# Expert results of a two-layer trunk: rows stored to DRAM and fetched per token, in place of scatter products into a transposed sum

## The chip, the cores and the metric

One core of a Trainium2 chip. The metric is the time of one execution on the device in microseconds (us), the median of several runs. All data are float32.

## What is computed

A trunk of two layers over 264 tokens (256 of a prompt, 8 single ones), 1024 channels. The change touches only the last stage, the mixture of experts: each token goes to the two best of eight experts, its results are weighted and added to the residual, and a last RMS norm follows.

```python
def swiglu(h, wg, wu, wd):
    return (jax.nn.silu(h @ wg) * (h @ wu)) @ wd

def moe_swiglu(h, router, wg, wu, wd):
    logits = (h @ router).astype(jnp.float32)
    top_v, top_i = lax.top_k(logits, TOP_K)
    gates = jax.nn.softmax(top_v, axis=-1)
    out = jnp.zeros_like(h)
    for e in range(N_EXPERTS):
        gate_e = jnp.sum(jnp.where(top_i == e, gates, 0.0), axis=-1)[..., None].astype(h.dtype)
        out = out + gate_e * swiglu(h, wg[e], wu[e], wd[e])
    return out
...
            x = x + mix
            x = x + moe_swiglu(rmsnorm(x, p['norm_ffn_odd'][i]), p['moe_router'][i], p['moe_w_gate'][i],
                               p['moe_w_up'][i], p['moe_w_down'][i])
    y = rmsnorm(x, p['final_norm'])
```

Each expert has gate and up weights of 1024 x 2816 and down weights of 2816 x 1024.

## The kernel before

The engines run programs of their own and meet at semaphores that are written out by hand. The expert stage is a sequence of items, one expert each: `moe_item(s, t)` with `s` from 0 to 6 written out, and `s` = 7 (`STATIC`) in a loop whose count comes from the routing; with this data the loop runs once. An item has a fixed number of slots for tokens, `SEQ_CAP` = 64, 96, 64, 96, 64, 128, 64, 64, and the experts are put in an order in which they fit.

**Weights.** SyncE loads an expert as 24 pieces (`load_piece`, L617): 8 for gate, 8 for up (1.44 MB each), 8 for down. They go round a ring of 33792 columns x 128 partitions. A piece of the second half of an expert is loaded over pieces of the first half, and so on, each load waiting on `w_used`, which PE raises when it has done with a piece (`LAST_OVER`).

**An item on PE.** Eight gate chunks (L2278, L2272 or L2264, by the number of slots), with work for other items slipped in between them: after chunk 1 the transposes of this item's gates and three small products that give the token numbers of the next item (`turn_gates`, L2172 and L2177, into bank 4); after chunks 2 to 5 one block each of `scatter` (L2200, L2208 or L2211). Then eight up chunks, transposes of the activations (L2299), transposes of the next item's rows (L2163), and the down products (L2317, L2328), whose result lies by slot: rows are tokens, columns are channels.

**What becomes of a result.** ScalarE and VectorE copy it out of PSUM into `ysb` (L1093, L1683, L1685). The next item's `scatter` multiplies it with the one-hot gate matrix `SelGT` (and `SelXT` where the item had 96 slots), so that a product of 128 channels x 264 tokens comes out, weighted. VectorE adds eight of these per item to `accT`, the transposed residual (`scattered`, L1636 and L1638). In the last item `sum_rows` (L2219) transposes `accT` back into the banks of `LAST_BANK` between up and down pieces. They stay open there (`mark_sums`, L2225, tells the accumulation state), and after the loop PE adds the last item's result on top (L2408). ScalarE squares the banks and VectorE writes the normed output from them.

**Rows.** The normed tokens stand in DRAM as `hrows`. For each next item VectorE writes the token numbers to `rowidx` (L1619) and POOL fetches the rows with an indirect DMA (`fetch_rows`, L784).

Of the kernel before, what the change touches and what calls it, by code (L numbers as in the profile page):

```python
# [32 lines left out]
SCAT = DC // 2  # L33
# [185 lines left out]
def bank_uses():  # L219
# [3 lines left out]
    for s in range(EXP + 1):  # L223
# [9 lines left out]
        item["selT"] = use(4, 5) if s and SEQ_CAP[s - 1] == 96 else use(4)  # L233
        if s:
            item["scat"] = use(4, 5)
            for _ in range(SCAT - 1):
                use(4, 5)
# [7 lines left out]
STEP5 = USES[EXP]["start"][1] - USES[EXP - 1]["start"][1]  # L245
EXIT_BASE = [sum(len(EXITS[SEQ_CAP[k]]) for k in range(s)) for s in range(EXP)]
# [5 lines left out]
def build(nc, i, o):  # L252
# [5 lines left out]
    with ctx:  # L258
# [185 lines left out]
        SelX = reg(19136, BLK * P).rearrange("p (k j) -> p k j", k=BLK)  # L444
        SelXT = reg(19520, BLK * P)
        iota32 = reg(20416, P)
# [3 lines left out]
        rowidx = sb("rowidx", 1, I32)  # L450
        hrows = nc.dram_tensor("hrows", [T, D], F32).ap()

# [66 lines left out]
        def _(sp):  # L519
# [99 lines left out]
            def first_expert():  # L619

                of = weights_of(slice(FIRST_EXPERT, FIRST_EXPERT + 1))
                for at in EARLY:
# [4 lines left out]
                    if at == RING_PIECES - 1:  # L627
                        sp.wait_ge(sem("t_full4"), 1)
                        sp.wait_ge(sem("t_full5"), 1)
                        sp.wait_ge(sem("hrows_stored"), 48)  # L630
# [23 lines left out]
            sp.wait_ge(sem("ord_ready"), 2)  # L654
# [15 lines left out]
        def _(pool):  # L670
# [3 lines left out]
            def then(ins):  # L674
# [32 lines left out]
                            pattern=[[0, DC], [-1, P]], channel_multiplier=1).then_inc(sem("wsn_ready"), 1)  # L707
# [50 lines left out]
            g.iota(iota32, pattern=[[0, 4], [1, P // 4]], base=64, channel_multiplier=0,  # L758
                   allow_small_or_imprecise_dtypes=True).then_inc(sem("route_const"), 1)
# [46 lines left out]
        def _(act):  # L806
# [28 lines left out]
            act.wait_ge(sem("wsn_ready"), 1)  # L835
# [29 lines left out]
            a.activation(arep, arep, ACT.Exp).then_inc(sem("arep_exp"), 1)  # L865
# [8 lines left out]
            a.activation(dtx[0:TS, 16:32], adt[0:TS, 32:48], ACT.Exp).then_inc(sem("sda_ready"), 1)  # L874
# [41 lines left out]
            act.wait_ge(sem("tot_ready"), 2)  # L916
# [30 lines left out]
            a.activation(Z, Z, ACT.Silu).then_inc(sem("z_ready"), 1)  # L947
# [96 lines left out]
            for k in range(BLK):  # L1044
                act.dma_start(hrows[P * k:P * k + ROWS[k], :], htok[0:ROWS[k], k, :]).then_inc(sem("hrows_stored"), 16)

# [6 lines left out]
            def moe_item(s, t):  # L1053
# [29 lines left out]

                for part in EXITS[cap]:
# [1358 lines left out]
```

## Time and profile before

| | |
|---|---|
| time, median of 3 runs | 1320.86 us (1320.65 to 1324.37) |
| the profiled execution | 1327.41 us, its span 1325.7 us |
| mean granted clock of TensorE | 0.987 of full speed |
| PE busy | 1299.6 us, 98% |
| VectorE, ScalarE, POOL busy | 373.8, 169.9, 61.0 us |
| DMA moved | 380.81 MB, mean 287 GB/s |
| gate and up products for 64 slots (L2278) | 280.9 us, 1792 instructions |
| down products (L2317) | 176.1 us, 704 instructions |
| adds into `accT` (L1636) | 12.0 us, 28 instructions, 429 ns each |

PE is the matmul queue. Each float32 product is recorded as two instructions. The ends of matmuls are modelled, so that an engine shown as busy may in part be waiting. The DMA share is the mean share of time in which the core's 16 DMA engines move something, GB/s what they moved. The queue q1 carries SyncE's loads, q10 ScalarE's DMAs, q0 those of POOL. The expert stage fills the second half of the span, from about 658 us on; its items begin on PE at 658, 721, 820, 886, 985, 1051, 1172 and 1241 us.

### The profile page before, as it was taken

Reading aid. Unit: us, or ns where it says so; the run is one execution under the profiler, and the core shown is the slowest. Engines: PE = TensorE matmul, PEld = TensorE weight load, DVE = VectorE, ACT = ScalarE, POOL = GpSimd, SP = SyncE. Lnnn points to the kernel's source line nnn. Section 1 sums busy time; section 2 is a strip of 40 time slices with the busy share of each in tenths; the row PEclk is TensorE's granted clock in tenths of the full one; section 3 lists DMA queues with packets and bytes.
Section 4 is the critical chain, followed back from the end, with each engine's and each line's share of the span. In section 5 each row is a group of like instructions: output and inputs, shape, how many; then the busy total and the mean of one; then the engine's idle time right before and its main releaser. Section 6 shows DMA issues by size and latency. Waiting matters only on the chain.

```text
span 1325.7 us, 17071 instructions
## 1 busy us (share of the span) xinstructions
PE 1299.6 (98%) x7217; PEld 826.4 (62%) x7217; DVE 373.8 (28%) x869; ACT 169.9 (13%) x367; POOL 61.0 (5%) x87
## 2 busy tenths in 40 slices
PE   8999999999999999999999999999999999999997
PEld 6878788888888888867843433434334444444452
DVE  5537775421111113984400110011100110110101
ACT  2241423010000100013200000000000000101002
POOL 1013110000000201100000000000000000000000
PEclk8999999999999999999799999999999999999999
DMA  8639633565456424354699999999999999899994
GB/s 289 206 130 304 221 96 96 191 179 168 127 166 223 143 72 127 132 198 197 267 388 424 408 424 425 408 424 410 424 425 424 424 406 425 323 359 418 409 423 188
DMA packets 105484, 380.81 MB, mean 287 GB/s; under 512 B 7580, under 2 KB 62796, under 8 KB 80778
## 3 DMA queue, kind: packets, MB, share of 16 engines
q1 hardware_dynamic: 97811, 359.46, 69.9%
q0 software_dynamic: 3216, 11.54, 2.7%
q10 hardware_dynamic: 4386, 8.76, 2.1%
q8 instruction: 57, 0.93, 0.3%
q14 instruction: 14, 0.11, 0.0%
HBM read 371.96 MB, written 8.86 MB: 287 GB/s over the span
## 4 chain that ended last, share of the span: by engine, by line
PE 89%; DVE 7%; ACT 1%; DMA 1%; SPq 1%; issue 1%; DVEq 0%; ACTq 0%
PE ps L1746 30%; PE ps L2278 21%; PE ps L2317 13%; PE ps L2264 6%; PE ps L2272 3%; DVE both L1450 3%; PE ps L1999 3%; PE ps L2328 2%; PE ps L2299 1%; PE ps L1991 1%; PE ps L1977 1%; PE ps L2211 1%; PE ps L2148 1%; PE ps L2200 1%; DMA both<-in_w_in_even_dram 1%
## 5 line engine op out<-in xcount | busy, mean ns | idle before, releaser
L1746 PE MATMUL ps<-both 128*128 128x264 f32 x2080 | 474.3, 390 | 0.5 <-DMA both<-in_w_in_even_dram 0.3
L1746 PEld LDWEIGHTS ps<-both 128*128 128x128 f32 x2080 | 397.0, 192 | 72.3 <-issue 2.7
L2278 PE MATMUL ps<-both 128*64 128x384 f32 (+1 forms) x1792 | 280.9, 466 | 0.8 <-ACT both L1050 0.8
L2278 PEld LDWEIGHTS ps<-both 128*64 128x64 f32 x1792 | 127.0, 138 | 152.6 <-issue 142.7
L2317 PE MATMUL ps<-both 128*64 128x512 f32 (+1 forms) x704 | 176.1, 596 | 0.0
L2317 PEld LDWEIGHTS ps<-both 128*64 128x64 f32 (+1 forms) x704 | 58.5, 143 | 98.6 <-issue 97.8
L1653 DVE TENSOR_TENSOR both<-both,ps 128x384 f32<-128x384 f32 (+7 forms) x46 | 20.9, 485 | 233.2 <-PE ps L2278 118.1
L2264 PE MATMUL ps<-both 128*128 128x510 f32 (+1 forms) x192 | 77.2, 559 | 0.0
L2264 PEld LDWEIGHTS ps<-both 128*128 128x128 f32 x192 | 35.9, 189 | 39.8 <-issue 32.5
L1450 DVE SCALAR_TENSOR_TENSOR both<-both,par 128x256 f32<-128x256 f32 x120 | 50.9, 481 | 1.0
L2272 PE MATMUL ps<-both 128*32 128x384 f32 (+1 forms) x512 | 47.1, 465 | 0.0
L1064 ACT ACTIVATE both<-ps 128x384 f32<-128x384 f32 (+7 forms) x46 | 19.0, 437 | 213.9 <-PE ps L2278 113.2
L1081 ACT ACTIVATE both<-ps 128x384 f32<-128x384 f32 (+1 forms) x28 | 12.5, 463 | 185.7 <-PE ps L2299 185.6
L784 POOL DMA_INDIRECT both<-hrows,rowidx x8 | 8.5, 1058 | 602.5 <-DVE rowidx L1619 345.0
L1999 PE MATMUL ps<-both 128*128 128x264 f32 x160 | 35.8, 386 | 0.0
L1636 DVE TENSOR_TENSOR both<-both,ps 128x264 f32<-128x264 f32 x28 | 12.0, 429 | 82.4 <-PE ps L2211 52.7
L1393 DVE TENSOR_TENSOR both<-both,ps 128x264 f32<-128x264 f32 x16 | 6.9, 429 | 99.9 <-PE ps L1746 70.0
L1999 PEld LDWEIGHTS ps<-both 128*128 128x128 f32 x160 | 30.4, 190 | 5.2
L1685 DVE COPY both<-ps 64x512 f32<-64x512 f32 x5 | 3.5, 694 | 101.9 <-PE ps L2317 101.9
L818 ACT ACTIVATE both<-both 128x264 f32<-128x264 f32 x32 | 12.8, 419 | 144.2 <-DVE both L1393 114.6
L1683 DVE COPY both<-ps 128x512 f32<-128x512 f32 x3 | 2.1, 692 | 98.8 <-PE ps L2328 60.8
L2272 PEld LDWEIGHTS ps<-both 128*32 128x32 f32 x512 | 14.3, 109 | 23.8 <-issue 22.7
(369 smaller groups left out, 882.4 us busy)
## 6 DMA issues: line engine op xcount, KB each, us to landing
both<-in_moe_w_gate_dram SPq DMA_DIRECT2D x64, 1408.0 KB
both<-in_moe_w_up_dram SPq DMA_DIRECT2D x64, 1408.0 KB
both<-in_moe_w_down_dram SPq DMA_DIRECT2D x48, 1536.0 KB
both<-in_w_in_even_dram SPq DMA_DIRECT2D x10, 2048.0 KB
both<-in_moe_w_down_dram SPq DMA_DIRECT2D x16, 1024.0 KB
both<-in_ffn_w_gate_dram SPq DMA_DIRECT2D x11, 1024.0 KB
both<-in_ffn_w_up_dram SPq DMA_DIRECT2D x11, 1024.0 KB
both<-in_ffn_w_down_dram SPq DMA_DIRECT2D x4, 2816.0 KB
```

Source lines behind the costliest of these rows:

```text
L1064: a.activation(act_view(p0, p1, r, a0, nb, q0, q1), exit_view(GATE_BANKS[cap][bank], p0, p1, nb, q0, q1, at), ACT.Silu).then_inc(sem("moe_ ...
L1450: ins = v.scalar_tensor_tensor(out=dst, in0=ca[:, c, k:k + TP], scalar=col("conf_dw_w", 8 * k + c), in1=dst, op0=ALU.mult, op1=ALU.add)
L1653: v.tensor_tensor(to, to, exit_view(UP_BANKS[cap][bank], p0, p1, nb, q0, q1, at), ALU.mult).then_inc(sem("moe_mul"), 1)
L1746: ins = mm(ps[:, 0:T], w[:, c, cols:cols + P], src[:, c, :], start=c == 0, stop=c == nk - 1)
L1977: mm(psum[at % RING][:, 0:T], w[:, c, P * (n % 2):P * (n % 2) + P], mix[:, c, :], start=c == DC, stop=False)
L1991: ins = mm(ahead[n][:, 0:T], out_w[n][:, c, P * (n % 2):P * (n % 2) + P], mix[:, c, :], start=False, stop=c == DC - 1)
L1999: ins = mm(ps[:, 0:T], w[:, c, P * (n % 2):P * (n % 2) + P], mix[:, c, :], start=c == DC, stop=c == DC - 1)
L2264: ins = mm(ps[:, 0:n], xg[:, c, 0:P], w[:, HALF * r + first:HALF * r + first + n], start=c == 0, stop=c == DC - 1)
L2272: ins = mm(ps[rows:rows + 32, 0:WIDE[k]], xg[:, c, 64:96], w[:, first:first + WIDE[k]], start=c == 0, stop=c == DC - 1)
L2278: ins = mm(ps[64 * r:64 * r + 64, 0:WIDE[k]], xg[:, c, 0:64], w[:, first:first + WIDE[k]], start=c == 0, stop=c == DC - 1)
L2317: ins = mm(out, lhsT, w[:, b - b0, 512 * h:512 * (h + 1)], start=b + r == 0, stop=b + r == 11)
L2328: ins = mm(psum[7][at:at + 32, :], hT32[:, k % 2, b - b0, k // 2, r, :], ws[r][:, b - b0, 512 * h:512 * (h + 1)], start=b == 0, stop=b == 10)
```

## The change

The results of items 0 to 6 no longer pass through scatter products.

- **Store.** When `ysb` holds an item's result, ScalarE stores it to a new DRAM buffer `yrows`, unweighted: one DMA of 128 rows for the item with 128 slots, two of 64 half rows for 64 slots, four for 96. A row of zeros stands at its start. The next overwriting of `ysb` waits for these stores (`y_put`). The result of an item with 96 slots is folded together on ScalarE and VectorE first.
- **Choice.** After item 0 VectorE works out for each token the two rows of `yrows` that hold its results, and their gates (`results_chosen`); a token whose expert is item 7 gets the zero row there.
- **Fetch.** POOL fetches them by six indirect DMAs (`fetch_results`), two rounds over 128, 128 and 8 tokens, ahead of its last fetch of rows. The first round waits for item 6's store, each DMA of the second for the adds of the first.
- **Add.** VectorE adds them, weighted, to `sums`, the residual by token, before it enters its loop for item 7 (`results_added`).
- **Residual.** PE transposes `accT` in items 0 to 2 after gate chunk 3 (`turn_sums`), and ScalarE and VectorE copy it to `sums`. `sum_rows` and `mark_sums` go.
- **Item 7.** Its gates are transposed after up chunk 1. Its six products stand at the end of the loop's body and open the banks anew; VectorE adds them to `sums`, and the squares and the output are taken from `sums`.
- Gate matrices are built for item 7 alone. `iota32` and `SelXT` go, and several semaphores of earlier stages are merged into others with the same order of work.

```diff
+            def fetch_results(m, k):
+
+                n, at = ROWS[k], 1 + BLK * m + k
+                if m:
+                    pool.wait_ge(sem("y_added"), k + 1)
+                pool.indirect_dma_start(
+                    out=yback[k][0:n, :], out_offset=None, in_=yrows[:, :],
+                    in_offset=bass.IndirectOffsetOnAxis(ap=rowidx[0:n, at:at + 1], axis=0)).then_inc(sem("y_back"), 16)
+
             pool.wait_ge(sem("crw_stored"), 32)
-            pool.wait_ge(sem("hrows_stored"), 48)
+            pool.wait_ge(sem("hrows_stored"), 64)
             for s in range(STATIC):
                 fetch_rows(s, 0)
-            pool.wait_ge(sem("ord_ready"), 2)
+            pool.wait_ge(sem("y_chosen"), 1)
+            pool.wait_ge(sem("y_put"), PUT_BASE[STATIC])
+            for m in range(2):
+                for k in range(BLK):
+                    fetch_results(m, k)
+            pool.wait_ge(sem("ord_ready"), 3)
             items = pool.value_load(tint[0:1, 0:1], min_val=1, max_val=ITEMS)
             with pool.Fori(0, items) as t:
                 fetch_rows(STATIC, t)
...
+                if s:
+                    act.wait_ge(sem("y_put"), PUT_BASE[s])
                 a.activation(ysb[0:n, 0:512], psum[6][0:n, :], ACT.Copy).then_inc(sem("ysb_lo"), 1)
+                if cap == 96:
+                    for h in range(2):
+                        a.activation(ysb[64 * h:64 * h + 32, 512:1024], psum[7][64 * h + 32:64 * h + 64, :],
+                                     ACT.Copy).then_inc(sem("ysb_lo"), 1)
+                if s < STATIC:
+                    act.wait_ge(sem("ysb_lo"), LO_BASE[s + 1])
+                    act.wait_ge(sem("ysb_hi"), s + 1)
+                    first = ROW_BASE[s]
+                    if cap == P:
+                        act.dma_start(yrows[first:first + P, :], ysb[:, :]).then_inc(sem("y_put"), 16)
+                    else:
+                        for h in range(2):
+                            act.dma_start(yrows[first:first + 64, 512 * h:512 * h + 512],
+                                          ysb[64 * h:64 * h + 64, 0:512]).then_inc(sem("y_put"), 16)
...
+            def results_added():
+
+                dve.wait_ge(sem("t_free4"), USES[BLK - 1]["res"][0] + 1)
+                dve.wait_ge(sem("t_free5"), USES[BLK - 1]["res"][1] + 1)
+                n = 0
+                for m in range(2):
+                    dve.wait_ge(sem("y_back"), 48 * (m + 1))
+                    if m:
+                        dve.wait_ge(sem("y_added"), BLK)
+                        dve.wait_ge(sem("sums_added"), BLK)
+                    for k in range(BLK):
+                        rows = ROWS[k]
+                        for h in range(2):
+                            to = sums[k][h][0:rows, :]
+                            v.scalar_tensor_tensor(out=to, in0=yback[k][0:rows, 512 * h:512 * h + 512],
+                                                   scalar=gsel[0:rows, 3 * m + k:3 * m + k + 1], in1=to, op0=ALU.mult,
+                                                   op1=ALU.add).then_inc(sem("y_added" if h else "sums_added"), 1)
...
+                dve.wait_ge(sem("t_full4"), t * STEP4 + (USES[s]["ids"][0] + 1))
+                rows_known(s, t)
+                dve.wait_ge(sem("rows_known"), t + (s + 1))
+                dve.sem_inc(sem("t_free4"), 1)
...
-                    scattered(t * STEP4 + USES[s]["scat"][0], t * STEP5 + USES[s]["scat"][1])
...
+                if s == STATIC:
+                    gates_turned(t * STEP4 + USES[s]["gates"][0])
...
+                    dve.wait_ge(sem("banks_read"), t * 6 + 6)
+                    for k in range(BLK):
+                        n = ROWS[k]
+                        for h in range(2):
+                            dve.wait_ge(sem("psum_full"), t * 6 + (len(TILES) + 2 * k + h + 1))
+                            to = sums[k][h][0:n, :]
+                            v.tensor_tensor(to, to, psum[LAST_BANK[k][h]][0:n, :], ALU.add).then_inc(
+                                sem("banks_read"), 1)
...
+            results_added()
+            dve.wait_ge(sem("y_added"), 2 * BLK)
+            dve.wait_ge(sem("sums_added"), 2 * BLK)
             items = dve.value_load(tint[0:1, 0:1], min_val=1, max_val=ITEMS)
             with dve.Fori(0, items) as t:
                 moe_item(STATIC, t)
...
+                for h, count in enumerate((n4, n5)):
+                    pe.wait_ge(sem(f"t_free{4 + h}"), count)
+                    for j in range(4):
+                        ins = tr(psum[4 + h][0:n, P * j:P * (j + 1)], accT[:, 4 * h + j, P * k:P * k + n], ident[:, :])
+                    ins.then_inc(sem(f"t_full{4 + h}"), 1)
...
-                    if s and 2 <= c < 2 + SCAT:
-                        scatter(SEQ_CAP[s - 1], t + s, t * STEP4 + USES[s]["selT"][0], t * STEP4 + USES[s]["scat"][0],
-                                t * STEP5 + USES[s]["scat"][1], (c - 2,))
+                        row_ids(SEQ_CAP[min(s + 1, EXP - 1)], t + (s + 2), t * STEP4 + USES[s]["ids"][0])
+                    if c == 3 and s < BLK:
+                        turn_sums(s, *USES[s]["res"])
                 for c in range(DC):
                     chunk(1, c)
                     if s == STATIC and c == 1:
-                        pe.wait_ge(sem("t_free4"), t * STEP4 + (USES[s]["scat"][0] + SCAT))
-                        pe.wait_ge(sem("t_free5"), t * STEP5 + (USES[s]["scat"][1] + SCAT))
-                        pe.wait_ge(sem("moe_silu"), t * XEXITS + (EXIT_BASE[s] + 4))
-                        sum_rows(0, 1)
-                    if s == STATIC and c == 2:
-                        sum_rows(1, 1)
+                        turn_gates(t + 1, t * STEP4 + USES[s]["gates"][0])
...
+                if s == STATIC:
+                    pe.wait_ge(sem("t_free5"), t * STEP5 + (USES[s]["gather"][1] + 1))
+                    pe.wait_ge(sem("t_free4"), t * STEP4 + (USES[s]["gates"][0] + 1))
+                    pe.wait_ge(sem("ysb_lo"), t + (LO_BASE[s] + 1))
+                    pe.wait_ge(sem("ysb_hi"), t + (s + 1))
+                    for k in range(BLK):
+                        n = ROWS[k]
+                        for h in range(2):
+                            mm(psum[LAST_BANK[k][h]][0:n, :], SelGT[64 * h:64 * h + 64, P * k:P * k + n],
+                               ysb[64 * h:64 * h + 64, 0:512], start=True, stop=True).then_inc(sem("psum_full"), 1)
```

## Rows read from the trace of the kernel before

**Rows 1.** Page, part 2: DMA share in 40 slices of the span, in tenths.

```profile
DMA  8639633565456424354699999999999999899994
```

**Rows 2.** Windows by item: us, busy by engine, PEclk, DMA share, GB/s.

```profile
984.80:1051.20 66.40, 66.40 (x408) 29.91 (x408) 8.80 (x23) 4.63 (x10) 0.96 (x1) 1.00 1.01 425
1051.20:1172.40 121.20, 121.20 (x337) 57.56 (x339) 10.21 (x31) 7.68 (x23) 0.94 (x1) 1.00 0.94 380
1172.40:1238.00 65.60, 65.52 (x388) 29.36 (x388) 8.46 (x23) 4.44 (x11) 0.93 (x1) 1.00 1.00 410
1238.00:1312.20 74.20, 73.39 (x457) 35.49 (x457) 8.03 (x22) 4.49 (x10) 0.96 (x1) 1.00 0.91 374
```

**Rows 3.** Timeline of PE, item 2: start us, us, operation, count.

```profile
828.44 1.16 PE L2200 MATMUL ps<-both 64*128 64x264 f32 x8
829.53 2.59 PE L2278 MATMUL ps<-both 128*64 128x384 f32 x16
```

**Rows 4.** Timeline of PE in item 5, and the chain of work there.

```profile
1060.67 0.49 PE L2172 MATMUL ps<-ident,both 128*128 128x128 f32 x3
...
1066.45 0.72 PE L2211 MATMUL ps<-both 64*128 64x264 f32 x4
...
1072.02 0.72 PE L2211 MATMUL ps<-both 64*128 64x264 f32 x4
...
1083.88 47.46 PE ps L2264 x120
```

**Rows 5.** Page, part 3: packets, MB, share of 16 engines' span.

```profile
q0 software_dynamic: 3216, 11.54, 2.7%
q10 hardware_dynamic: 4386, 8.76, 2.1%
```

**Rows 6.** Windows of 20 and 12 us around row fetches, columns as before.

```profile
700.00:720.00 20.00, 20.00 (x101) 7.09 (x100) 0.56 (x1) 1.96 (x5) 0.00 (x0) 1.00 1.01 424
720.00:740.00 20.00, 20.00 (x161) 8.54 (x159) 4.92 (x16) 0.59 (x1) 1.83 (x1) 1.00 1.01 400
990.00:1002.00 12.00, 12.00 (x85) 6.24 (x85) 3.96 (x14) 0.00 (x0) 0.96 (x1) 1.00 1.01 422
```

**Rows 7.** POOL's row fetches: their line, and the time to landing.

```profile
L784 POOL DMA_INDIRECT both<-hrows,rowidx x8: 907/952/1832, 667.2 to 1248.2; - x8
...
DMA to landing us min/median/max: 8.5/8.9/9.8
```

**Rows 8.** Windows at the end of the weight stream, columns as before.

```profile
1304.00:1305.00 1.00, 1.00 (x10) 0.83 (x10) 0.00 (x0) 0.00 (x0) 0.00 (x0) 1.00 0.64 270
1305.00:1306.00 1.00, 1.00 (x6) 0.29 (x4) 0.00 (x0) 0.00 (x0) 0.00 (x0) 1.00 0.20 82
```

**Rows 9.** Timeline of the end, from PE's last piece to the last store.

```profile
1310.28 1.94 PE L2317 MATMUL ps<-both 128*64 128x512 f32 x8
...
1312.27 0.69 DVE L1685 COPY both<-ps 64x512 f32<-64x512 f32 x1 [23.37 <-PE ps L2317]
...
1313.60 2.95 PE L2408 MATMUL ps<-both 64*128 64x512 f32 x12
...
1314.76 0.60 ACT L1110 ACTIVATE both<-ps 128x512 f32<-128x512 f32 x1 [0.39 <-PE ps L2408]
...
1315.56 0.15 DVE L1704 TENSOR_SCALAR both<-both 128x1 f32<-128x1 f32 x1 [2.02 <-ACT both L1110]
...
1316.59 1.41 DVE L1711 SCALAR_TENSOR_TENSOR both<-ps,both 128x512 f32<-128x512 f32 x2
...
1322.16 0.34 SPq L666 DMA_DIRECT2D out_y_sample_dram<-both  x1
```

**Rows 10.** Timeline of PE, item 7: the first group of sums.

```profile
1268.96 1.16 PE L2219 MATMUL ps<-ident,both 128*128 128x128 f32 x8
```

**Rows 11.** Windows of PE at the lower clock: us, busy, PEclk, DMA, GB/s.

```profile
646.00:662.00 16.00, 15.22 (x65) 0.50 0.89 350
1322.00:1324.00 2.00, 0.00 (x0) 0.50 0.23 61
```

More of the change, by code:

```diff
@@ L32 @@
 XROUNDS = 4
-SCAT = DC // 2
 PIECES = 24
@@ L232, in bank_uses @@
         item = {"start": tuple(at)}
[L233 to L237, printed above, removed]
+        item["ids"] = use(4)
+        if s < BLK:
+            item["res"] = use(4, 5)
+        if s >= STATIC:
+            item["gates"] = use(4)
         item["gather"] = use(4, 5)
@@ L245 @@
 STEP5 = USES[EXP]["start"][1] - USES[EXP - 1]["start"][1]
+ROW_BASE = [1 + sum(SEQ_CAP[:s]) for s in range(STATIC)]
+YROWS = 1 + sum(SEQ_CAP[:STATIC])
+PUTS = {64: 2, 96: 4, P: 1}
+PUT_BASE = [16 * sum(PUTS[SEQ_CAP[k]] for k in range(s)) for s in range(EXP)]
+LO_BASE = [sum(3 if SEQ_CAP[k] == 96 else 1 for k in range(s)) for s in range(EXP)]
 EXIT_BASE = [sum(len(EXITS[SEQ_CAP[k]]) for k in range(s)) for s in range(EXP)]
@@ L1082, in columns @@
                     ins.then_inc(sem("ht_ready"), 1)
+                if s < BLK:
+                    if s == 0:
+                        act.wait_ge(sem("hrows_stored"), 64)
+                        act.wait_ge(sem("crw_stored"), 32)
+                    act.wait_ge(sem("t_full4"), USES[s]["res"][0] + 1)
+                    n = ROWS[s]
+                    a.activation(sums[s][0][0:n, :], psum[4][0:n, :], ACT.Copy).then_inc(sem("t_free4"), 1)
                 for part in EXITS[cap]:
@@ L1108, in _ @@
                 for h in range(2):
[L1109 to L1110 removed]
+                    act.wait_ge(sem("banks_read"), items * 6 + (2 * k + h + 1))
+                    a.activation(fsq[0:n, 512 * h:512 * (h + 1)], sums[k][h][0:n, :], ACT.Square,
                                  accum_out=ssum[0:n, 2 * k + h:2 * k + h + 1]).then_inc(sem("fin_sq"), 1)
@@ L1698, in _ @@
                 moe_item(STATIC, t)
-            gates_turned(items * STEP4 + (USES[EXP]["start"][0] - STEP4))
             dve.wait_ge(sem("fgain_loaded"), 16)
@@ L2215, in sum_rows @@
-            def sum_rows(k, h):
-                n = ROWS[k]
-                for j in range(4):
-                    mm(psum[LAST_BANK[k][h]][0:n, P * j:P * (j + 1)], accT[:, 4 * h + j, P * k:P * k + n], ident[:, :],
-                       start=j == 0, stop=False)
-            def mark_sums(opened):
-                for b, n in ((0, P), (1, P), (2, P), (3, P), (7, TS)):
-                    mm(psum[b][0:n, 0:1], ones[0:1, 0:n], ones[0:1, 0:1], start=opened, stop=not opened)
+                pe.wait_ge(sem("sel_ready"), chosen)
@@ new lines, in row_ids, with turn_gates @@
+                for b in range(BLK):
+                    ins = mm(psum[4][0:cap, BLK * P:BLK * P + 1], Sel[:, b, 0:cap], tokid[:, b:b + 1], start=b == 0,
+                             stop=b == BLK - 1)
+                ins.then_inc(sem("t_full4"), 1)
+            def turn_gates(value, n4):
+                pe.wait_ge(sem("t_free4"), n4)
+                pe.wait_ge(sem("selg_ready"), value)
+                for b in range(BLK):
+                    ins = tr(psum[4][:, P * b:P * (b + 1)], SelG[:, b, :], ident[:, :])
+                ins.then_inc(sem("t_full4"), 1)
@@ L2301, in turn_act, with down @@
                     ins.then_inc(sem("t_act"), 1)
-                def down(k, between=None):
+                def down(k):
                     b0, b1 = SEGS[k]
```

234 lines of the change are left out of this document (90 added, 144 removed).

## The prediction

> **What bounds the kernel now.** I read the page first: PE is busy for 98% of the span, but a busy PE in this profile may still be waiting inside a matmul, so this settles nothing. The line of DMA shares is full from the 20th slice on [rows 1]. Both could bound the expert part. So next came a table of windows cut where PE changes from one item (one expert with its slots) to the next [rows 2]. It gives DMA at a share of 1.01 and 410 to 425 GB/s in every item but the sixth (`s` = 5, 128 slots), where it falls to 380.
>
> Then I counted bytes backwards. One expert's weights are 3 x 1024 x 2816 x 4 B = 34.6 MB. After 1051.2 us the windows move 380 x 121.2 + 410 x 65.6 + 374 x 74.2 = 100.7 MB, of which 0.8 MB are three row fetches, so 99.9 MB of weights. Items 5 to 7 need 103.8 MB. At PE's start of item 5 the weight stream is thus only 3.9 MB ahead. By the same count it is 10.8 MB ahead at 984.8, 15.1 MB at 1172.4 and 7.1 MB at 1238.0. The ring holds 33792 columns, 17.3 MB. So DMA runs without a gap up to item 5. In item 5 PE needs 121.2 us where the stream needs 34.6/0.425 = 81 us, the ring fills, and SyncE can load only what PE releases. After that the stream is full again to its last byte, near 1305.3 [rows 8].
>
> PE's timeline says the other half. In item 2 a block of scatter products takes a slot of 829.53 - 828.44 = 1.09 us [rows 3] and otherwise the chunks follow each other evenly. PE never shows a gap for weights. So today PE sets the time, with the stream just behind it. There are two tight places, the start of item 5 and the end. How tight: of the 3.9 MB, 1.44 MB are the first piece itself, and the other 2.5 MB are 5.8 us at 425 GB/s. At the end PE's last piece, 1.94 us long, starts at 1310.28 [rows 9], 5.0 us after the stream's last byte. From both comes the time between a piece's last byte and PE's start. The trace bounds it by the last output store, from its issue at 1322.16 to the end of the span at 1325.7, 3.5 us with the issue in it, and by nothing from below. I take 2.5, nearer to the one row there is. Slack: 3.3 us at item 5, 2.5 us at the end.
>
> The Trainium skill, "DMA: Bandwidth & Descriptors", section "Anatomy of one DMA", gives about 2.0 us of fixed cost, mostly the wait until the last byte is confirmed. By that the two slacks would be 3.8 and 3.0 us, and the result 1 us lower.
>
> **Part by part, PE.** Removed are four scatter blocks in each of items 1 to 7. The block costs 5.57 us from one block to the next against 4.75 us for a bare chunk in item 5 [rows 4], so 0.8 us, and 1.1 us where the item before had 96 or 128 slots. That is 16 x 0.8 + 12 x 1.1 = 26 us, with the gate transposes of items 1 to 6 (about 0.4 us each, rows 4) and six groups of sums at about 1.1 us [rows 10] about 35 us. Added are eight transposes of `accT` in each of items 0 to 2, 1.1 us each time by the same row, and one gate transpose in item 7. If PE alone set the time this would be -30 us.
>
> It isn't, since the stream can't be hurried. Before item 5 PE gains about 14 us over items 0 to 4 but may use only the 3.3 us of slack: term **-3.3**. Item 5 itself stays bound by PE (about 117 us against 81), and there the removal counts in full: 4 x 0.82 + 0.42 for the three gate transposes [rows 4]: **-3.7**. Items 6 and 7 follow the stream again, whose restart hangs on PE's releases in item 5, so what PE saves in them gives only the slack at the end: **-2.5**.
>
> **DMA.** Stored are 576 rows of 4 KB, 2.36 MB, fetched 528 rows, 2.16 MB. Items 0 to 3 store 320 rows, 1.31 MB, ahead of item 5: full price. Item 4's 64 rows fall into item 5, where the stream waits for PE: free. Item 5's 128 rows (0.52 MB) come at its end, where the stream is still partly waiting: half. Item 6's 64 rows (0.26 MB) and all fetches fall into item 7, where it is full. That makes 1.83 MB of stores and 2.16 MB of fetches at some price p per MB. The lowest is the full rate, 1/0.425 = 2.35 us. The highest is from a fetch of 64 rows, where the 20 us around it moved 400 instead of 424 GB/s [rows 6]: 0.48 MB lost and 0.26 MB moved, 1.75 us for 0.26 MB, 6.7 us per MB. A fetch of 128 rows (990 to 1002) moved 422 against 425, so it cost 2.5 us per MB, and four of the six new fetches are of 128 rows. Between them lie the queues' own shares [rows 5]: ACT's queue, which will carry the stores, 2.1% of 1325.7 us for 8.76 MB, 3.2 us per MB; POOL's queue 2.7% for 11.54 MB, 3.1. I take these, since they are near the 128-row fetch and leave something for the 64-row pieces. 1.83 x 3.2 + 2.16 x 3.1 = **+12.6**.
>
> The Trainium skill's same page, section "Specifications", puts the SBUF side of DMA at 435 GB/s at most; the stream already has 425. By that rule the new bytes come on top at 2.3 us per MB and the sum below would be +2.3 instead of +5.7. It speaks against this change as the rows do.
>
> **The end.** Today PE goes from the last piece over 0.64 us of transposes to six final products, ACT squares each from PSUM, and DVE writes the first output at 1316.59. In the change the transposes are gone, but DVE must first add all six product tiles into `sums`, and the output steps stand behind all six in its queue. From PE's end at 1312.2: copy out to 1312.96, first product ready 1.16 us later [rows 9], six adds at 0.70 us (as L1711 and L1685 take) to 1318.35, then 1.03 us from the half step to the first output: 1319.4 against 1316.59. The later outputs keep their pace. The adds for 8 tokens may be shorter, so I take **+2.6**.
>
> Sum: -3.3 - 3.7 - 2.5 + 12.6 + 2.6 = **+5.7 us** against the profiled execution (1327.41 us, span 1325.7). The runs shown have a median of 1320.86, 6.5 less, and I put the same difference on it: **1326.6 us**.
>
> **Taken at nothing.** VectorE loses 56 adds and gains about 14 small steps after item 0; it idles for most of each item. Its wait for `y_back` is the exception, below. ScalarE's stores wait for VectorE's copy, and behind them stands only the next item's SiLU, a whole gate stage later. The waits on `y_put` are for stores tens of us old. The folding of the 96-slot result costs some 2 us on ACT and DVE, and the next item wants those banks later than that. POOL's fetches stand ahead of its fetch of rows for item 7's successor, whose result PE wants only after the up stage. Renamed semaphores cost nothing. The entry of the loop loses a 3 us marking step, hidden behind the stream.
>
> **Rivals.** (1) *The bytes slip in.* With p the whole sum is -6.9 + 3.99 p. It turns negative below p = 1.7 us per MB. That happens if writes to DRAM go beside reads, and fetched rows use gaps that a share of 1.01 doesn't show. At p = 0: -6.9, **1314.0**. For it: stores are the first large writes in this stage, and no row shows one under a full stream. Against: no fetch cost less than the full rate. Chance 0.17.
> (2) *Dear bytes.* All at the 64-row price, +19.8, **1340.7**; only the stores of 64 and 96 rows (1.57 MB) at it, +5.5 more, **1332.1**. For it: those stores use half of the partitions, as that fetch did. Chance 0.13.
> (3) *PE waits for the fetched rows.* In item 7 DVE adds all fetched rows before it frees bank 4, and PE wants the bank behind the second up chunk. PE ends item 6 near 1230; copy and store some 5.5 us; three issues of 1 us and 8.9 us to landing [rows 7], and some 2 more since 1.06 MB share the queue: 1250; first adds and the second round about 15 us more; adds 4.2 us: 1270. PE comes there with the stream at about 1265 and has 43.2 - 5.5 = 37.7 us of work behind it [rows 10], so it ends at 1308.6 with the new transposes, before the 1315.3 of my sum (1312.2 + 5.7 - 2.6). A wait of over 5 us may also cost clock: after PE's last product the granted clock falls to half, 0.50 in 1322 to 1324 [rows 11], 1.2 instead of 2.4 GHz. It stood there from 646 to 662 too, which would cost 8 us of PE work if all of such a stretch were needed; half of that I put to this case, and PE ends at 1312.6. The Trainium skill's "TensorE: Matmul & The Clock Gate", Part 1, says as much, that idleness brings the gate back to half rate. So the wait decides from a chain about 3 us longer than mine; 8 us longer gives 1320.6 for PE, 5.3 above the sum, **1331.9**. Chance 0.13.
> (4) *The change does not act*, for instance since the stream turns out not to be near its limit on both sides: about 1321, 0.03.
>
> **How the numbers follow.** My own case has 0.54, with p from 2.35 to 4.5 and the unknown latency from 0 to 3.5 us: 1319 to 1332. About 0.15 of it lies within 0.3% (4 us, about what a measurement of this kernel can tell from no change). Slower 0.39 + 0.13 + 0.13 = 0.65; within 0.15 + 0.03 + 0.03 = 0.21; faster 0.14. The range goes down into rival 1 and up over the milder form of rival 2: 1316 to 1336.
>
> **What would show it.** Item 5 takes 117 to 118 us instead of 121.2 and starts within 2 us of its old time, while items 2 and 4 show chunks spread to the stream's 3.4 us. The stream's last byte comes 4 to 8 us later, PE's last piece follows it by about 4.5 us, and the first output comes 7.2 us after PE's end instead of 4.4. Total DMA bytes rise by 4.5 MB. I am wrong if item 5 starts several us earlier than now (cheap stores), if PE shows a gap over 5 us early in item 7's up stage, or if PE's chunks stay at 2.4 us in item 4.

## The result, and the profile after

| | before | after |
|---|---|---|
| time, median | 1320.96 us (4 runs) | 1333.84 us (1331.44 to 1335.12, 4 runs) |
| ratio after / before | | 1.0089, 95% interval 1.0067 to 1.0112 |
| the profiled execution | 1327.41 us, span 1325.7 us | 1334.46 us, span 1332.7 us |
| mean granted clock | 0.987 | 0.983 |
| PE busy | 1299.6 us | 1263.3 us |
| DMA moved | 380.81 MB | 385.31 MB |

The change costs 12.9 us by the medians, 11.8 by the ratio; the forecast was 5.7 us, to 1326.6. PE's busy time fell by 36 us and the time still went up. Of these 36 us, 8 belong to the first profile of the kernel before: in the second one, below, PE is busy for 1291.5 us. So 28 us went, where the prediction counted about 30 net.

The page of the changed kernel, packets, MB and share of the 16 DMA engines by queue (before: [rows 5]). The new bytes stand where they were expected, 2.16 MB on POOL's queue and 2.37 MB on ScalarE's.

```profile
DMA  8639533574455433363899999999999999999992
...
q0 software_dynamic: 3856, 13.70, 3.1%
q10 hardware_dynamic: 5684, 11.13, 2.6%
```

Windows by item of the changed kernel, columns as in [rows 2]. The first row has the bounds of item 4 in the kernel before; in the changed kernel item 4 starts on PE at 975.0 us, and items 5, 6 and 7 at 1047.7, 1165.3 and 1225.1.

```profile
984.80:1051.20 66.40, 56.91 (x316) 23.19 (x313) 3.38 (x6) 4.62 (x10) 0.00 (x0) 1.00 1.01 425
1047.40:1165.00 117.60, 117.25 (x316) 56.27 (x316) 5.23 (x17) 7.08 (x21) 0.90 (x1) 1.00 0.99 403
1165.00:1225.00 60.00, 60.00 (x370) 35.43 (x371) 3.85 (x10) 4.42 (x10) 0.89 (x1) 1.00 1.01 408
1225.00:1316.70 91.70, 67.43 (x382) 29.77 (x378) 13.39 (x26) 4.58 (x10) 6.79 (x7) 0.87 0.89 363
```

The first row, most of it item 4, now shows PE waiting for the stream (of weights), 56.91 us busy of 66.40: PE begins the item nearly 10 us earlier than before and gives most of this back in waits. Item 5 takes 117.5 us where it took 121.2, as forecast. Item 6 is 5.6 us shorter too, 60.0 against 65.6. Then the last row: 24 us of 91.7 without PE, while the DMA share is not full either. What happens there stands in the waits of PE (line, what it waited for, us in total, times, longest) and in the chain of work that ended last (start us, us):

```profile
PE ps L2273 <- DVE both L1737: 18.8, 1, 18.8
PE ps L2373 <- DMA both<-in_moe_w_down_dram: 7.3, 12, 0.8
```

```profile
1216.52 8.76 PE ps L2373 x40
1226.56 9.42 DMA yrows<-both
1239.38 12.73 DMA both<-yrows,rowidx
1256.76 13.07 DMA both<-yrows,rowidx
1269.86 4.06 DVE both L1710 x6
1277.44 16.38 PE ps L2334 x96
```

PE stands still for 18.8 us at the last item's gate transposes (L2273), released by the gate matrices (L1737), which stand behind the second round of adds (L1710) in VectorE's program. The chain leads back over two rounds of fetches and the store of item 6's result. This is rival 3 of the prediction, with a chance of 0.13, and the time is within 2 us of the one it was given, 1331.9.

VectorE in the same stretch (timeline: start us, us, line, operation, [idle before <-releaser]), and POOL's fetches with their time to landing:

```profile
1252.25 4.05 DVE L1710 SCALAR_TENSOR_TENSOR both<-both 128x512 f32<-128x512 f32 x6 [26.26 <-DMA both<-yrows,rowidx]
1269.86 4.05 DVE L1710 SCALAR_TENSOR_TENSOR both<-both 128x512 f32<-128x512 f32 x6 [13.56 <-DMA both<-yrows,rowidx]
...
1275.63 0.86 DVE L1737 TENSOR_SCALAR both<-iota,both 128x128 f32<-128x128 f32 x3 [0.32 <-DVE rowidx L1671]
```

```profile
L804 POOL DMA_INDIRECT both<-yrows,rowidx x6: 885/946/1229, 1236.9 to 1256.8; - x6
```

The end of the changed kernel, against [rows 9]: the first row is the second half of PE's last down piece, which begins at 1314.8 and ends at 1316.7; the first output is written at 1323.11, and the last store is issued at 1328.70.

```profile
1315.70 1.03 PE L2373 MATMUL ps<-both 128*64 128x512 f32 x4
...
1318.76 3.67 DVE L1773 TENSOR_TENSOR both<-both,ps 128x512 f32<-128x512 f32 x6 [1.28 <-PE ps L2421]
...
1323.11 1.42 DVE L1804 SCALAR_TENSOR_TENSOR both<-both 128x512 f32<-128x512 f32 x2
...
1328.70 0.34 SPq L675 DMA_DIRECT2D out_y_sample_dram<-both  x1
```

### The profile page after: what moved, and what is told of

Same layout as the page of the kernel before. It is cut to its first block, busy times and chain, and to the rows that moved or that the text cites. A ratio compares the mean times of both kernels' runs of the same rounds, so it can differ in the third digit from the quotient of the medians.

```text
span 1332.7 us, 16652 instructions
## 1 busy us (share of the span) xinstructions
PE 1263.3 (95%) x7002; PEld 809.8 (61%) x7002; DVE 358.6 (27%) x814; ACT 174.3 (13%) x374; POOL 66.0 (5%) x108
## 2 busy tenths in 40 slices
DMA packets 107421, 385.31 MB, mean 289 GB/s; under 512 B 7965, under 2 KB 63181, under 8 KB 82716
## 4 chain that ended last, share of the span: by engine, by line
PE 77%; DMA 11%; DVE 7%; SPq 1%; ACT 1%; issue 1%; POOL 0%; DVEq 0%; ACTq 0%; POOLq 0%
PE ps L1839 30%; PE ps L2334 15%; PE ps L2373 10%; PE ps L2320 6%; DMA both<-in_moe_w_gate_dram 5%; PE ps L2328 3%; DVE both L1502 3%; PE ps L2092 3%; DMA both<-in_moe_w_up_dram 2%; DMA both<-yrows,rowidx 2%; PE ps L2382 2%; PE ps L2355 1%; PE ps L2084 1%; PE ps L2070 1%; DMA yrows<-both 1%
## 5 line engine op out<-in xcount | busy, mean ns | idle before, releaser
L2334 PEld LDWEIGHTS ps<-both 128*64 128x64 f32 x1792 | 136.6, 138 | 160.2 <-issue 125.2
L1445 DVE TENSOR_TENSOR both<-both,ps 128x264 f32<-128x264 f32 x16 | 6.9, 429 | 99.9 <-PE ps L1839 70.0
L843 ACT ACTIVATE both<-both 128x264 f32<-128x264 f32 x32 | 12.8, 419 | 144.4 <-DVE both L1445 114.6
L1000 ACT ACTIVATE both<-both 128x264 f32<-128x264 f32 x22 | 9.3, 423 | 139.3 <-DVE both L1474 139.3
L1464 DVE TENSOR_TENSOR both<-ps,rstd 128x264 f32<-128x264 f32 x22 | 9.5, 433 | 66.4 <-PE ps L1839 66.4
```

Of the source, the lines that this page charges most:

```text
L2334: ins = mm(ps[64 * r:64 * r + 64, 0:WIDE[k]], xg[:, c, 0:64], w[:, first:first + WIDE[k]], start=c == 0, stop=c == DC - 1)
```

## The experiments

Two theories at first. A: bytes and wait both count; the sum of the forecast holds, +5 to 6 us, and the wait puts its 6 to 7 us on top. B: one of the two is the whole loss, the other is hidden behind it.

**The kernel before, once more**, for a second profile: in the first one the granted clock was at half for 17 us at 646 us.

> The kernel before, unchanged, profiled once more. Its first profiled execution took 1327.4 us against a median of 1321, and shows 17 us at half clock from 646 us on, which the profile of the changed kernel does not have; there item 0 starts on PE at 651.6 instead of 658.1 us. Theory 'clock luck': the low stretch is not a property of the kernel; a second profile has none, its item 0 starts near 651.6 and its span is about 1319 us, so that the true distance of the two kernels in spans is some 13 us and not 7. Rival: the stretch belongs to the kernel before, and the changed kernel is free of it since some of its early steps moved; then the second profile has it again at 646 us and a span near 1325.7.

Measured: 1321.27 us (1318.57 to 1324.82), ratio 0.9987 [0.9972, 1.0002], and a span of 1320.1 us in its profile, 5.6 less than the first profile of the same kernel. The window that stood at PEclk 0.50 in [rows 11]:

```profile
646.00:662.00 16.00, 15.22 (x110) 9.11 (x111) 7.74 (x46) 3.16 (x4) 0.98 (x1) 1.00 0.83 320
```

Item 0 starts on PE at 649.2 instead of 658.1, item 5 at 1043.9 instead of 1051.1. So the profile on which the forecast rests was a late one by some 6 to 7 us. In this one PE already waits for weights at the start of item 5:

```profile
PE ps L2264 <- DMA both<-in_moe_w_gate_dram: 1.5, 1, 1.5
```

This profile is the one to compare the others with. Its chain of work, item 5's start, item 6's start and the last product and store:

```profile
1043.87 9.69 PE ps L2264 x24
...
1165.08 4.88 PE ps L2278 x32
```

```profile
1304.70 1.94 PE L2317 MATMUL ps<-both 128*64 128x512 f32 x8
...
1316.59 0.34 SPq L666 DMA_DIRECT2D out_y_sample_dram<-both  x1
```

**The wait taken away** (`split_adds`): the second round's adds go into item 7's work, behind the gate matrices.

```diff
-            def results_added():
+            def results_added(rounds):
...
-                for m in range(2):
+                for m in rounds:
...
                 moe_xg(SEQ_CAP[min(s + 1, EXP - 1)], t * STEP5 + USES[s]["gather"][1])
+                if s == STATIC:
+                    results_added((1,))
+                    dve.wait_ge(sem("y_added"), 2 * BLK)
+                    dve.wait_ge(sem("sums_added"), 2 * BLK)
...
-            results_added()
-            dve.wait_ge(sem("y_added"), 2 * BLK)
-            dve.wait_ge(sem("sums_added"), 2 * BLK)
+            results_added((0,))
```

> The changed kernel with only the order on VectorE changed: the adds of the second fetched round stand late in item 7, behind the copy of the next rows, and not ahead of the item. Same bytes, same adds. Theory 'PE waits' : PE reaches the gate transposes at 1257.7 us and waits to 1276.5 for VectorE; the first round is added by 1256.3, so the wait falls to about 1 us, PE follows the stream, whose last byte comes at 1306.3, and ends at 1306.3 + 2.5 + 1.9 = 1310.7 instead of 1316.7: -6 us, about 1328 us. The half clock of 1261 to 1281 goes as well. Rival 'bytes': the stream with its new bytes sets the end and the wait is hidden: within 1 us of 1333.8.

Measured: 1327.86 us (1323.83 to 1329.13), ratio 1.0038 [1.0023, 1.0052]. The wait is gone from PE's list, which is led by waits for weights, and the chain of work ends in the stream:

```profile
PE ps L2335 <- DMA both<-in_moe_w_up_dram: 16.5, 16, 3.3
PE ps L2374 <- DMA both<-in_moe_w_down_dram: 10.0, 16, 0.8
PE ps L2335 <- DMA both<-in_moe_w_gate_dram: 6.0, 5, 2.1
```

```profile
1045.43 9.69 PE ps L2321 x24
...
1162.94 4.88 PE ps L2335 x32
...
1225.35 42.86 DMA both<-in_moe_w_up_dram
1270.94 36.19 DMA both<-in_moe_w_down_dram
```

```profile
1307.18 1.94 PE L2374 MATMUL ps<-both 128*64 128x512 f32 x8 [0.40 <-DMA both<-in_moe_w_down_dram]
...
1321.10 0.34 SPq L675 DMA_DIRECT2D out_y_sample_dram<-both  x1
```

Taking the wait away, and the half clock that came with it, is worth 1333.8 - 1327.9 = 6.0 us (6.7 by the ratios). Theory A holds. What is left, by these rows against those of the kernel before: item 5 starts 1.6 later, takes 3.7 less, from item 6's start to the last product 4.6 more (144.2 against 139.6), from there to the last store 2.0 more (13.9 against 11.9). Sum +4.5; by the ratio it is +5.0.

**The fetches left out** (`no_fetch`) **and all new bytes left out** (`no_bytes`).

```diff
             for s in range(STATIC):
                 fetch_rows(s, 0)
-            pool.wait_ge(sem("y_chosen"), 1)
             pool.wait_ge(sem("y_put"), PUT_BASE[STATIC])
-            for m in range(2):
-                for k in range(BLK):
-                    fetch_results(m, k)
...
-            results_added()
-            dve.wait_ge(sem("y_added"), 2 * BLK)
-            dve.wait_ge(sem("sums_added"), 2 * BLK)
+            dve.wait_ge(sem("t_free4"), USES[BLK - 1]["res"][0] + 1)
+            dve.wait_ge(sem("t_free5"), USES[BLK - 1]["res"][1] + 1)
```

> The changed kernel without the six fetches and without their adds; the stores stay. The results of items 0 to 6 are left out of the output. Theory: the wait goes and 2.16 MB leave the full stream. At 2.35 to 3.1 us per MB the last byte comes 5.1 to 6.7 us earlier than 1306.3, and PE ends near 1304 to 1306 instead of 1316.7: 1321 to 1323 us. If a fetched MB costs 6.7 us, as a fetch of 64 rows did, the stream ends 14 us earlier and the time is 1314 to 1316. If fetched bytes are free, it is 1328, as with the adds split.

In the second kernel ScalarE's stores to `yrows` and the waits on `y_put` are gone as well. Both leave the results of items 0 to 6 out of the output.

> The changed kernel with neither stores nor fetches nor adds of fetched rows (the results of items 0 to 6 are left out of the output). Compared with the one without fetches it gives the price of the stores alone. Theory (3.2 us per MB for the 1.31 MB ahead of item 5, and about 0.5 MB behind it): 4 to 6 us less than without fetches, 1316 to 1318 us, with item 5 starting some 4 us before its 1047.7. Rival 'stores slip in beside reads': item 5 starts at the same time and the time is within 1.5 us of the one without fetches.

Measured: `no_fetch` 1319.35 us (1317.28 to 1322.29), ratio 0.9977 [0.9961, 0.9994]; `no_bytes` 1315.76 us (1314.03 to 1317.99), ratio 0.9950 [0.9936, 0.9963]. The last product of the down stage in each:

```profile
1300.70 1.94 PE L2368 MATMUL ps<-both 128*64 128x512 f32 x8 [0.39 <-DMA both<-in_moe_w_down_dram]
```

```profile
1295.24 1.94 PE L2350 MATMUL ps<-both 128*64 128x512 f32 x8 [0.40 <-DMA both<-in_moe_w_down_dram]
```

Between `split_adds` and `no_fetch` lie 6.5 us of the last product's start, and 8.5 us of the medians: 3.0 to 3.9 us for each of 2.16 MB. The 1321 to 1323 us that were expected put the fetches too low. Between `no_fetch` and `no_bytes` lie 5.5 us by the product and 3.6 us by the medians for the stores, 1.5 to 2.3 us for each of 2.36 MB. All new bytes together: 11.9 us by the product, 12.1 by the medians, where the forecast had 12.6. Rival 1, in which the bytes cost next to nothing, is refuted, and without its bytes the change would be a gain of 5.5 us (by the ratio 6.6).

**Where PE's removed work counts.** `ballast_others` and `ballast_item5` give back to PE, in `split_adds`, 16 products of 128 x 128 that nobody reads, once in five items around item 5 and once in item 5.

```diff
                     chunk(1, c)
+                    if s in (1, 2, 3, 4, 6) and 2 <= c < 6:
+                        if s < BLK and c == 2:
+                            pe.wait_ge(sem("t_free5"), USES[s]["res"][1] + 1)
+                        for _ in range(4):
+                            mm(psum[5][:, 0:P], ident[:, :], ones[:, :], start=True, stop=True)
```

> split_adds with the PE work of the removed scatter products given back in items 1, 2, 3, 4 and 6 only: in each, 16 products of 128 x 128 that nobody reads, four behind each of the third to sixth up chunks (about 1.1 us for four, so some 4.4 us an item, 22 us in all). If PE in these items waits for the stream of weights anyway, as the windows of the items say, the 22 us lie in its waits: the time stays within 1 us of split_adds, 1327.9, and item 6 starts within 1 us of 1163. The rival, in which PE is what sets the pace there and the removed products were worth their duration, gives 1327.9 + up to 22 = 1345 to 1350; every us of start of item 6 above 1163 is a us of PE that counted.

In the other kernel the first added line reads `if s == 5 and 2 <= c < 6:`.

> split_adds with the same 16 products in item 5 alone, the one item whose duration went from 121.2 to 117.5 us with the change. If item 5 is PE-bound, as the forecast has it, it takes 117.5 + 3.5 to 4.4 = 121 to 122 us, and the kernel 1331.4 to 1332.3. The rival, that item 5 had become bound by the stream (its DMA share is 0.99) and only part of the removed work was gained, gives item 5 117.5 to 119 us and the kernel 1328 to 1329.5.

Measured: `ballast_others` 1326.66 us (1326.23 to 1326.83), ratio 1.0049 [1.0032, 1.0065]; `ballast_item5` 1330.39 us (1328.17 to 1333.04), ratio 1.0083 [1.0062, 1.0105]. Five times as much work outside item 5 moves nothing that can be told from `split_adds`; it goes into PE's waits, which shrink:

```profile
PE ps L2335 <- DMA both<-in_moe_w_up_dram: 8.6, 4, 2.9
...
PE ps L2374 <- DMA both<-in_moe_w_down_dram: 2.1, 4, 0.8
```

In item 5 it costs 2.5 us against `split_adds` and 3.7 against `ballast_others` by the medians (4.5 to 5.9 by the ratios; its four runs lie at 1328.2, 1328.3, 1332.5 and 1333.0, so the size is loose), and the item takes 121.1 us instead of 117.5. The reason is that in this item the ring is full and the stream may load only what PE releases: between 1047 and 1165 us of `split_adds` SyncE's loads wait 95 of 118 us for PE to release pieces, between 1225 and 1306 only 8.6 of 81. So a slower PE slows the loads, as the window of the item shows, first `split_adds`, then `ballast_item5` (columns as in [rows 2]): 390 GB/s instead of 402.

```profile
1047.00:1165.00 118.00, 118.00 (x327) 56.45 (x327) 5.91 (x18) 7.67 (x22) 0.90 (x1) 1.00 0.98 402
```

```profile
1047.00:1165.00 118.00, 118.00 (x342) 58.40 (x340) 5.22 (x17) 7.07 (x21) 0.90 (x1) 1.00 0.97 390
```

**Does it matter when the bytes come?** `rest_first` fetches the results from items up to 5 while item 6 runs.

```diff
-                n, at = ROWS[k], 1 + BLK * m + k
+                n, at = ROWS[k], 1 + BLK * (1 - m) + k
...
-            pool.wait_ge(sem("y_put"), PUT_BASE[STATIC])
             for m in range(2):
+                pool.wait_ge(sem("y_put"), PUT_BASE[STATIC - 1 + m])
...
+                if s == STATIC - 1:
+                    results_added((0,))
+                if s == STATIC:
+                    results_added((1,))
```

> Same stores and same fetched bytes as split_adds, but the round that needs no row of item 6 (each token's result from an item up to 5) is fetched and added already while item 6 runs, and only the other round waits for item 6's store and is added late in item 7. By the theory that only bytes are left to pay once PE waits for no added row, it gives the time of split_adds, 1327.9, within 1 us, with the fetch packets of the first round in item 6. The rival, that the burst of fetches behind item 6 delays the last item's weights more than the same bytes earlier do, gives 1323 to 1326.

Measured: 1326.48 us (1324.97 to 1327.89), ratio 1.0047 [1.0030, 1.0064]. The first round of fetches was issued from 1177.7 us on instead of 1234.6, the second at 1231.9 instead of 1251.8, and the time is that of `split_adds`, so no cost of the burst behind item 6 shows once PE doesn't wait for it.

**PE kept busy during the wait** (`wait_busy`, from the changed kernel):

```diff
                     if s == STATIC and c == 1:
+                        for _ in range(64):
+                            mm(psum[5][:, 0:P], ident[:, :], ones[:, :], start=True, stop=True)
                         turn_gates(t + 1, t * STEP4 + USES[s]["gates"][0])
```

> The changed kernel with 64 products of 128 x 128 that nobody reads ahead of the last item's gate transposes, where PE stands still for 18.8 us until the fetched rows are added; they take 17.4 us at the full clock. The wait itself stays as long, since its end is set by the fetches. If the granted clock of 0.50 after the wait (1261.0 to 1281.5 us in the changed kernel) is a matter of PE having stood still, it goes, and with it the 4 us of work at half clock behind the wait: 1333.8 - 2 = 1331.8, or as much as 1 us more or less. If the whole loss is the wait, 1333.8 within 0.5. If the dummy products run past the wait's end, 0 to 3 us more.

Measured: 1334.43 us (1332.27 to 1335.13), ratio 1.0109 [1.0092, 1.0126]: no gain. PE's windows across the wait and just behind it (us, busy, PEclk, DMA share, GB/s), first the changed kernel, then this one:

```profile
1261.00:1277.00 16.00, 0.46 (x2) 0.50 1.02 412
1277.00:1282.00 5.00, 5.00 (x21) 0.55 1.01 384
```

```profile
1261.00:1276.00 15.00, 11.17 (x97) 0.97 1.01 411
1276.00:1279.00 3.00, 3.00 (x12) 0.58 0.98 409
```

With PE at work through most of the wait, the granted clock stayed up there, so the half clock of the changed kernel did come from PE standing still. But the products took 14.6 us, less than the 17.4 expected, PE then stood for another 3.8 us, and the clock fell for 3.4 us all the same, from 1275.1:

```profile
1256.67 14.56 PE L2400 MATMUL ps<-ones,ident 128*128 128x128 f32 x128
1275.06 0.89 PE L2273 MATMUL ps<-ident,both 128*128 128x128 f32 x3 [3.83 <-DVE both L1737]
```

So the kernel got back under 1 us of PE work, which the times can't show. How the 6.0 us of `split_adds` divide into wait and clock is therefore not shown. An estimate from rows of the changed kernel: PE ends its last piece at 1316.7, where the stream's last packet at 1306.8, 0.5 us to PE's start and 1.9 us of products would allow 1309.3, 7.4 us earlier; at most 2.5 of these are the 5.0 us that PE worked at half clock (1276.5 to 1281.5), and the rest is the wait.

**Bytes or rows?** `half_fetch` takes half of each row, beside another measurement of `split_adds`:

```diff
+        yhalf = yrows.rearrange("r (h c) -> (r h) c", h=2)
...
-                    out=yback[k][0:n, :], out_offset=None, in_=yrows[:, :],
+                    out=yback[k][0:n, 0:512], out_offset=None, in_=yhalf[:, :],
```

> split_adds once more, unchanged, as the comparison for half_fetch on the same chip: 1327.9 within 1 us, a ratio of 1.004 to 1.005.

> split_adds with each fetched row cut to its first 512 columns: as many row fetches on the same queue, but 2 KB instead of 4 KB each, 1.08 MB instead of 2.16 MB; both halves of a token's sum are made from this half, so the second half of the output holds other data. The stores stay whole. If what the fetches cost goes by bytes (3.0 us/MB at the end of the stream between split_adds and no_fetch), the stream ends 3.2 us earlier and the kernel takes 1323.6 to 1324.7. If it goes by the number of rows fetched, the time stays at 1327.9 within 1 us. The packets of 2 KB show which: half of the 134 to 144 ns of the 4 KB ones, or nearly as long.

Measured: `split_again` 1327.35 us (1326.22 to 1328.58), ratio 1.0038 [1.0025, 1.0050]; `half_fetch` 1323.01 us (1320.86 to 1327.73), ratio 1.0011 [0.9998, 1.0024]. Half of the fetched bytes are worth 4.3 us by the medians (3.6 by the ratios, known to some 2 us), about half of the 8.5 us that all of them cost. Had the number of rows set the price, it would have stayed at 1327.9. POOL's queue, `half_fetch`:

```profile
q0 software_dynamic: 3600, 12.62, 2.9%
```

It has 256 packets fewer. Of the fetches' packets only 16, those of the two fetches over 8 tokens, have 2 KB; the other 256 still have 4 KB, two half rows in one, so bytes and packets fell together. The experiment thus speaks for bytes, or packets, against rows. (A 4 KB packet of these fetches takes 159 ns in the median by the trace, not the 134 to 144 ns of the expectation, and the 2 KB ones 84 ns.)

No version here beats the kernel before. The fastest of those that leave nothing out are `split_adds` and `rest_first`, 0.4 to 0.5% slower than it.

## Why the prediction was right in direction and short in size

The measured time lies in the range of 1316 to 1336, but the likeliest case did not happen: a rival did, one that the prediction held for unlikely, and the upper bound came from another rival. So the number in the range is in part luck. Step by step:

**What bounds it: right.** The stream, with item 5 the one place where PE's work counts. The ballast shows both halves: 16 products in item 5 make the item 3.6 us longer, and 80 outside it nothing that shows in the time.

**Item 5's -3.7: right.** 117.5 against 121.2 us.

**Slack before item 5, -3.3: too much.** It was read from a profile in which 17 us at half clock had put PE late. In the second profile PE already waits 1.5 us for weights at that point, and without new bytes item 5 starts at 1042.3, only 1.6 us earlier.

**Slack at the end, -2.5: too little.** It rested on 2.5 us from a piece's last byte to PE, bounded by a single far row, and on a last byte at 1305.3 where the last packet in that profile ends at 1306.2. In `split_adds`, `no_fetch` and `no_bytes` the last packet ends at 1306.65, 1300.17 and 1294.71, and PE starts on the piece 0.53 us later each time. In the second profile of the kernel before, the last packet ends at 1298.23 and PE's last piece starts at 1304.70, so PE was 5.9 us behind what the stream allowed. The Trainium skill's "DMA: Bandwidth & Descriptors", section "Anatomy of one DMA", puts about 2 us of fixed cost on a DMA that GpSimd issues, mostly for confirming the last byte. For these weight loads, which SyncE issues, at most 0.5 us lies behind the recorded end of the last packet, so the slack that the prediction worked out by the page, 3.0 us, was too low as well.

**Bytes, +12.6: right in sum, 11.9 us.** Item 5's start with stores but without fetches or adds was 1045.5, against 1042.3: 3.2 us for the first 1.31 MB, where 4.2 was in the sum. That is one pair of profiles, and the starts of item 5 in the kernels with stores range from 1044.1 to 1048.4, so the split between the places is known to some 2 us only.

**The end, +2.6: 2.0.** From the last product to the last store 13.9 us against 11.9, in `no_bytes` as well (1295.24 to 1309.16). It is the price of the new order of the last steps, and neither of stores nor of fetches.

So the sum of the likeliest case, +5.7, measured +5.0 once the wait was out: 1327.9 against 1326.6. That it came so close is in part luck, since the two slacks were off by 1.7 and 3.4 us in opposite directions. Nor do the terms as measured add up to it: -1.6 - 3.7 - 5.9 + 11.9 + 2.0 = +2.7, against +4.5 by the rows. What is missing is that a gain in item 5 does not reach the end whole. Without the new bytes item 6 starts 5.3 us earlier than in the second profile of the kernel before (1159.8 against 1165.1), but the stream's last packet ends only 3.5 us earlier (1294.7 against 1298.2). Why is open.

**The step that failed is in rival 3: the chain in front of PE's wait.** Its mechanism was written down and its effect priced at 1331.9. Its length was put at 40 us and measured 51.4, so it was taken not to decide, and its chance was put too low:

| from item 6's end on PE | estimated, us | measured, us |
|---|---|---|
| copy and store, to POOL's first fetch | 5.5 | 11.8 |
| first round, to the first add | 14 to 15 | 15.4 |
| first adds and second round | 15 | 17.6 |
| adds | 4.2 | 4.1 |
| to the gate matrices' release of PE | 0 | 2.6 |
| sum | 40 | 51.4 |

Half of the error is one term: item 6's result, two DMAs of 128 KB, landed 9.4 us after the second was issued, under a full stream. No row of before showed a store there, and [rows 7] had 8.5 us for a fetch of that size; the estimate took less than the nearest row. A second error lay beside it. Item 6's end on PE was taken as 1230, while the removed work let PE get there at 1225.1; that moved both the chain's start and PE's arrival (1257.7 instead of 1265), and PE's arrival doesn't matter when the chain comes last. Of the 11.4 us of error the earlier start took back 4.9: the chain let PE go at 1276.5 instead of 1270, 6.5 us late, where by the prediction's own count 3 us were enough to decide. From the gate transposes' end PE had 39.2 us of work (37.7 estimated), up to 2.5 of them for the half clock, and the stream's last packet had ended 10 us before PE did, at 1306.8. That the rival's 1331.9 came near 1333.8 is partly luck too: it took the chain 8 us longer and 4 us for the clock.

**The base was off as well.** The profiled execution was 6.5 us above the median, and the prediction put "the same difference" on the result. Most of the difference goes with the half clock at 646: the second profile has none there, 8.1 us less of PE busy time, and a span 5.6 us shorter. The changed kernel's profile did not have it either, and shows 1334.5 beside a median of 1333.8. Taking the difference off was right; reading slacks off that profile was not.

**The marks.** Item 5 in 117 to 118 us: seen. Its start within 2 us of 1051.1: no, 1047.7. That is 3.4 us earlier, which was named as a sign of cheap stores, and a false one: against the second profile, 1043.9, it starts 3.9 us later. Item 4's chunks spread to 3.4 us: seen (1003.6 to 1007.0). PE's last piece 4.5 us behind the stream: neither, 8.0 in the changed kernel, because of the wait, and 0.5 in `split_adds`. DMA +4.5 MB: seen. The stream's last byte 4 to 8 us later: 8.6 against the second profile, 0.6 against the first. First output 7.2 us after PE's end: 6.4. A gap over 5 us early in item 7's up stage, named as a sign of being wrong: seen, 18.8 us.

## What to carry to other kernels

When results go through DRAM between the last two items of a pipeline, add up the whole latency chain (copy, store, fetch, add, fetch, add) with landing times from rows under the same DMA load, and compare it with the consumer's arrival; if they are within a few microseconds, put the adds behind the consumer's next need instead of ahead of it. Work saved on an engine is worth its time only where that engine holds up the stream, here in one item of eight, while bytes added to a stream are paid wherever it is full. Before reading slacks of a few microseconds off one profile, see whether it has a stretch of low clock ahead of them.

## What the runs showed of the hardware that was not expected

- One kernel, two profiles: 17 us of PE at half of the clock (1.2 instead of 2.4 GHz) in one and none in the other, 5.6 us of span between them. The Trainium skill's "TensorE: Matmul & The Clock Gate", Part 1, says that the cold time at a start differs from run to run; here it differs in the middle of the kernel too.
- In `wait_busy` the clock fell for 3.4 us from 1275.1, after a wait of only 3.8 us; in the changed kernel likewise from 1247.4, after 4 us (1243 to 1247) in which PE was busy for 1.93, with one wait of 2.07 us. What such short falls cost was not measured by itself.
- Under a full stream, of the three fetches in one burst the first (128 rows) took 9.5 and 9.8 us to land in the two rounds, like the single ones of [rows 7], the second (128 rows) 13.0 and 13.2, and the third, of only 8 rows, 12.7 and 13.1. So the third took 3 us longer than the first though it is far smaller, and its size can't be the reason. The two stores of 128 KB of item 6's result took 8.1 and 9.4 us.
- From the end of the last piece's last packet to PE's first product on it, where PE was waiting for it: 0.53 us in three kernels.
